# Filter spectra of a Hyena layer: three groups per order on TensorE in place of five, laid out by ScalarE, and an earlier second modulation trip

## What is computed

```python
def fft_long_conv(u, h, bias):
    L = u.shape[1]
    uf = u.astype(jnp.float32)
    spec = jnp.fft.rfft(uf, n=2 * L, axis=1) * jnp.fft.rfft(h, n=2 * L, axis=0)[None]
    y = jnp.fft.irfft(spec, n=2 * L, axis=1)[:, L // 2:L // 2 + L]
    return (y + uf * bias.astype(jnp.float32)).astype(u.dtype)

def hyena(u, conv_w, conv_b, w1, b1, w2, b2, w3, freq, bias):
    u = short_conv(u, conv_w, conv_b)
    v, x1, x2 = jnp.split(u, 3, axis=-1)
    h = implicit_filters(L, w1, b1, w2, b2, w3, freq)
    z = x1 * fft_long_conv(v, h[0], bias[0])
    return x2 * fft_long_conv(z, h[1], bias[1])

# per layer: scale, shift and gate vectors
mod_l = jnp.split(s_lat @ w_mod[l] + b_mod[l], N_MOD, axis=-1)
hl = modulate(rmsnorm(xl, norm1_g[l]), mod_l[0], mod_l[1])
```

## Time and profile before

| | us |
|---|---|
| time before, median of 3 runs (1947.94 to 1949.6) | 1948.33 |
| the profiled execution, its own time | 1946.0 |
| its span in the profile | 1944.1 |
| of it TensorE busy | 1884.3 (97%) |
| VectorE busy | 626.0 (32%) |
| ScalarE busy | 460.1 (24%) |

### The profile page before, as it was taken

The page is one execution under the profiler, slowest core; times in us unless marked ns, Lnnn a source line. Parts: engine busy times, 40 slices in busy tenths (PEclk is TensorE's granted clock), DMA queues, the critical chain, the costliest instruction groups (busy, mean ns, idle before and its releaser), DMA issues.

```text
span 1944.1 us, 43452 instructions
## 1 busy us (share of the span) xinstructions
PE 1884.3 (97%) x20106; PEld 1373.3 (71%) x20106; DVE 626.0 (32%) x892; ACT 460.1 (24%) x626; POOL 43.4 (2%) x53
## 2 busy tenths in 40 slices
PE   8999999999899999999998899999999999999997
PEld 3677776787688887776877886656666666666765
DVE  3545456444423332226645651001010111101012
ACT  4221144332433342114314441000000000000001
POOL 0000000002000001100000010000000000000000
PEclk9999999999999999999999998999999999999999
DMA  9721111126122326732332388999999999999991
GB/s 367 295 103 43 69 66 65 55 90 247 45 107 86 108 73 269 315 112 94 123 110 76 119 322 350 365 397 354 365 371 381 389 369 376 343 401 361 409 349 45
DMA packets 65489, 436.73 MB, mean 225 GB/s; under 512 B 7264, under 2 KB 8416, under 8 KB 21792
## 3 DMA queue, kind: packets, MB, share of 16 engines
q1 hardware_dynamic: 60992, 405.07, 54.6%
q0 software_dynamic: 4320, 28.96, 3.8%
HBM read 432.95 MB, written 1.05 MB: 223 GB/s over the span
## 4 chain that ended last, share of the span: by engine, by line
PE 87%; DVE 6%; DMA 3%; ACT 2%; issue 2%; SPq 0%; POOL 0%; DVEq 0%; ACTq 0%
PE psum L1878 24%; PE psum L1400 12%; PE psum L1923 11%; PE psum L1402 11%; PE psum L1401 11%; PE psum L1594 2%; PE psum L1447 2%; PE psum L1600 2%; DMA mod_units_e<-in_w_mod 1%; DVE squares L977 1%; PE psum L1518 1%; DVE h_lo L970 1%; PE psum L1635 1%; PE psum L1657 1%; PE psum L1853 1%
## 5 line engine op out<-in xcount | busy, mean ns | idle before, releaser
L1878 PE MATMUL psum<-expert_units,gathered 128*32 128x256 f32 (+1 forms) x9216 | 469.5, 363 | 1.1 <-issue 1.0
L1878 PEld LDWEIGHTS psum<-expert_units,gathered 128*32 128x32 f32 x9216 | 303.1, 110 | 154.9 <-issue 7.2
L1400 PE MATMUL psum<-h_hi,units_hi 128*128 128x512 f32 (+1 forms) x928 | 346.2, 373 | 13.0 <-DVE h_lo L970 5.9
L1402 PE MATMUL psum<-h_hi,units_lo 128*128 128x512 f32 (+1 forms) x928 | 334.9, 361 | 0.0
L1401 PE MATMUL psum<-h_lo,units_hi 128*128 128x512 f32 (+1 forms) x928 | 334.8, 361 | 0.0
L924 DVE TENSOR_TENSOR units_lo<-raw_units,units_hi 128x2048 fp32r<-128x2048 f32 (+2 forms) x88 | 175.1, 1991 | 322.4 <-ACT units_hi L564 322.3
L564 ACT ACTIVATE units_hi<-raw_units 128x2048 fp32r<-128x2048 f32 (+2 forms) x88 | 147.2, 1673 | 483.5 <-PE psum L1402 421.9
L1923 PE MATMUL psum<-expert_units,expert_midT 128*32 128x256 f32 x4080 | 225.3, 379 | 0.0
L1400 PEld LDWEIGHTS psum<-h_hi,units_hi 128*128 128x128 f32 x928 | 175.3, 189 | 53.2 <-issue 19.6
L1402 PEld LDWEIGHTS psum<-h_hi,units_lo 128*128 128x128 f32 x928 | 175.5, 189 | 27.2
L1923 PEld LDWEIGHTS psum<-expert_units,expert_midT 128*32 128x32 f32 x4080 | 135.8, 110 | 83.0 <-issue 1.0
(11 more groups left out here) (268 smaller groups left out, 2008.4 us busy)
## 6 DMA issues: line engine op xcount, KB each, us to landing
expert_units<-in_moe_up SPq DMA_DIRECT2D x128, 1024.0 KB, 8.1
expert_units<-in_moe_w SPq DMA_DIRECT2D x88, 1024.0 KB, 6.8
expert_units<-in_moe_up_rest SPq DMA_DIRECT2D x64, 768.0 KB, 5.1
raw_units<-in_w_in SPq DMA_DIRECT2D x40, 1024.0 KB, 4.9
raw_units<-in_ffn_w SPq DMA_DIRECT2D x22, 1024.0 KB, 4.9
mod_units<-in_w_mod POOLq DMA_DIRECT2D x20, 1024.0 KB, 10.4
raw_units<-in_ffn_w SPq DMA_DIRECT2D x16, 704.0 KB, 4.8
raw_units<-in_w_pab SPq DMA_DIRECT2D x16, 512.0 KB, 3.5
```

The lines of the kernel that those rows point to most:

```text
L1400: MM(o, wh, xh, start=first, stop=False)
L1402: return MM(o, wl, xh, start=False, stop=last)
L1878: ins = MM(o[GRP * q:GRP * (q + 1), :], G[:, k, at, GRP * s:GRP * (s + 1)], W[:, kk, c, :], start=k == 0 and rr % 2 == 0, stop=k == DK - 1 ...
```

## The change

Only three groups per order are computed on TensorE, six per layer: the real low bins (g = 0), the imaginary low bins with the Nyquist bin in row 0 (g = 1), and the high bins, real in the upper 64 rows and imaginary in the lower 64 (g = 2). ScalarE lays out the five tables from them in 8 instructions per order. The matrix `dftk` shrinks from 9 to 7 blocks of 64 columns (576 to 448 KB), the seventh being a column of ones with a zero in row 0, which is the scale that clears row 0 of table 1. TensorE's order in layer 0 becomes: spectra 0 and 1, trip 0, spectrum 2, turn 0, trip 1, spectrum 3, turn 1, spectra 4 and 5. ScalarE's order changes too. The wait for all copies ahead of `hyena_inputs` is split: layer 0 waits for two copies before it, both layers for four and for two copies after the first product, and for all of them after the stage.

```diff
             def spectrum_out(l, q):
-                act.wait_ge(f_pe, 11 * l + 4 + q)
-                A(spec[:, q // 5, q % 5, :], PS[:, spectrum_bank(l, q), :], ACT.Copy).then_inc(f_ac, 1)
+                act.wait_ge(f_pe, 7 * l + 4 + q)
+                o, g = q // 3, q % 3
+                bins = PS[:, spectrum_bank(l, q), :]
+                if g == 0:
+                    A(spec[:, o, 0, :], bins, ACT.Copy)
+                    A(spec[:, o, 2, :], bins, ACT.Copy).then_inc(f_ac, 1)
+                elif g == 1:
+                    A(spec[:, o, 1, :], bins, ACT.Identity, scale=dftks[l][:, 0, 6 * HALF:6 * HALF + 1])
+                    act.wait_ge(f_ac, 6 * l + 4 + q)
+                    A(spec[0:1, o, 2, :], bins[0:1, :], ACT.Copy).then_inc(f_ac, 1)
+                else:
+                    A(spec[0:HALF, o, 3, :], bins[0:HALF, :], ACT.Copy)
+                    A(spec[HALF:BINS, o, 3, :], bins[0:HALF, :], ACT.Copy)
+                    A(spec[0:HALF, o, 4, :], bins[HALF:BINS, :], ACT.Copy, scale=-1.0)
+                    A(spec[HALF:BINS, o, 4, :], bins[HALF:BINS, :], ACT.Copy).then_inc(f_ac, 1)
...
-                    for q in range(5):
+                    for q in range(4):
                         spectrum_out(0, q)
                     hi(0, 0, 0)
-                    for q in range(5, 7):
-                        spectrum_out(0, q)
+                    early = 4
+                else:
+                    spectrum_out(l, 0)
+                    norm_root(2)
+                    for q in range(1, 3):
+                        spectrum_out(l, q)
+                    early = 3
+                for q in range(early, 6):
+                    norm_hi(2 * l, SHIFT1, HH, 2 * (q - early), 2)
+                    spectrum_out(l, q)
+                norm_hi(2 * l, SHIFT1, HH, 2 * (6 - early), 6)
+                if l == 0:
                     hi(1, 1, 0)
-                    early = 7
-                else:
-                    for q in range(2):
-                        spectrum_out(l, q)
-                    norm_root(2)
-                    for q in range(2, 5):
-                        spectrum_out(l, q)
-                    early = 5
-                for q in range(early, 10):
-                    spectrum_out(l, q)
-                    norm_hi(2 * l, SHIFT1, HH, 2 * (q - early), 2)
-                norm_hi(2 * l, SHIFT1, HH, 2 * (10 - early))
+                norm_hi(2 * l, SHIFT1, HH, 2 * (9 - early))
...
@@ hyena_inputs, after the first product
+                    if n == 0:
+                        pe.wait_ge(f_ac, 4 + 6 * l + 4 - 2 * l)
...
@@ filter_spectra
-                    if l and q == 6:
-                        pe.wait_ge(evac, evb[0]["down"] + DK)
-                    reuse = 8 if l else 6
-                    if q >= reuse:
-                        pe.wait_ge(f_ac, 10 * l + 5 + q - reuse)
-                    o, g = q // 5, q % 5
+                    o, g = q // 3, q % 3
...
@@ TensorE's order in layer 0
             mod_turn(0, 0)
-            filter_spectra(0, 3, 6)
             mod_units(0, 1)
-            filter_spectra(0, 6, 7)
+            filter_spectra(0, 3, 4)
             mod_turn(0, 1)
-            filter_spectra(0, 7)
+            filter_spectra(0, 4)
...
-                pe.wait_ge(f_ac, 10 * l + 14)
+                if l == 0:
+                    pe.wait_ge(f_ac, 4 + 2)
                 hyena_inputs(l)
+                pe.wait_ge(f_ac, 4 + 6 * (l + 1))
```

More of the change, by code:

```diff
@@ L177, in build @@
         decays = [place("decay0", 59, [P, 2, 2, HY_W]), place("decay1", 88, [P, 2, 2, HY_W])]
[L178 removed]
+        dftks = [place("dft_filter0", 79, [P, 2, 7 * HALF]), place("dft_filter1", 96, [P, 2, 7 * HALF])]
         taps = place("filter_taps", 67, [P, 2, 2, HY_W])
@@ L1492, in filter_taps, with filter_spectra @@
                 last.then_inc(f_pe, 1)
-            def filter_spectra(l, first=0, end=10):
+            def filter_spectra(l, first=0, end=6):
                 for q in range(first, end):
@@ L1504, in filter_spectra @@
                         pe.wait_ge(n_rt, 2 * l + 1)
-                    if l and q == 6:
-                        pe.wait_ge(evac, evb[0]["down"] + DK)
-                    reuse = 8 if l else 6
-                    if q >= reuse:
-                        pe.wait_ge(f_ac, 10 * l + 5 + q - reuse)
-                    o, g = q // 5, q % 5
-                    for c in range(2):
-                        if g == 3:
-                            for h in range(2):
-                                last = MM(PS[h * HALF:(h + 1) * HALF, bank, :], dftks[l][:, c, 6 * HALF:7 * HALF], tapss[l][:, o, c, :],
-                                          start=c == 0, stop=c == 1)
-                        else:
-                            f = 7 * HALF if g == 4 else g * BINS
-                            last = MM(PS[:, bank, :], dftks[l][:, c, f:f + BINS], tapss[l][:, o, c, :],
-                                      start=c == 0, stop=c == 1)
+                    o, g = q // 3, q % 3
+                    for c in range(2):
+                        last = MM(PS[:, bank, :], dftks[l][:, c, g * BINS:(g + 1) * BINS], tapss[l][:, o, c, :],
+                                  start=c == 0, stop=c == 1)
                     last.then_inc(f_pe, 1)
@@ L2064, in tables @@
     imn[:, 0] = nyq
-    ren = re[:, :BINS].copy()
-    ren[:, 0] = nyq
     low, high = slice(0, BINS), slice(BINS, nbins)
     fwd = np.concatenate([re[:, low], imn[:, low], re[:, high], im[:, high], im[:, high], re[:, high]], axis=1)
-    fil = np.concatenate([re[:, low], (im * (k > 0))[:, low], ren, re[:, high], -im[:, high], im[:, high]], axis=1)
+    past_dc = np.repeat(np.arange(L) > 0, HALF).reshape(L, HALF)
+    fil = np.concatenate([re[:, low], imn[:, low], re[:, high], im[:, high], past_dc], axis=1)
     n = (np.arange(L) + L // 2)[None, :]
```

5 lines of the change are left out of this document (2 added, 3 removed).

## The result

The change makes the kernel slower. Its median is 1955.36 us over 10 executions (1950.82 to 1960.76) against 1948.49 for the kernel before, measured together with it (10 executions, 1945.65 to 1950.95); the ratio is 1.0033 [1.0023, 1.0043], the brackets being its 95% interval. A second batch gave 1953.30 against 1948.93, ratio 1.0030 [1.0019, 1.0041]. So the change costs 4 to 7 us; I had forecast 2.3, and 1953.1 as the upper end.

A forecast was written before the change was run, and what follows sets the result against it. It took VectorE's and ScalarE's chain of norm items as the bound, not TensorE. Layer 0 (0.5 + 2.3 + 1.2 = +4.0) and layer 1 (-3.0 + 1.3 = -1.7) gave +2.3: 1948.33 to 1950.6 us, range 1947.7 to 1953.1.

The forecast's parts named there:

- TensorE is not the bound: Both layers: the four groups saved, some 7.3 us of TensorE per layer, are worth nothing by themselves.
- Trip 1 waits for its fourth unit until 35.5, ends at 39.1: Layer 0: the fourth unit's load holds trip 1, so of 5.5 us earlier only 1.6 are left.
- hi of unit 0, +0.5: Layer 0, ScalarE: hi stands behind spectrum 3's copies, so VectorE's low of unit 0 starts at 44.0 in place of 43.50.
- ScalarE's copies: Layer 0, between norm items: copies of spectrum 4 cost 0.05, of spectrum 5 1.2; with hi of unit 1, +2.3 us.
- the wait ahead of item 10: Layer 0: hi of unit 1, moved between norm items 9 and 10, makes VectorE wait 1.05 us.
- the third rival: ScalarE's narrow copies are cheap, half of 0.59, so the median is 1948.4 us; chance 0.13.
- Layer 1, -3.0 and +1.3: Layer 1's norm chain starts 3.0 us earlier, and copies of spectra 4 and 5 among the items cost 1.3; net -1.7.
- The clock behind the first gap, +1.2: Layer 0: TensorE, nearly idle from 31.6 to 35.5, likelier than not falls to 1.2 GHz afterwards; +1.2 us, bounds 0 and 1.7.
- The second rival: Layer 0: the clock stays low through trip 1 and spectrum 3, costing 3.4 in place of 1.2; 1952.8 us, chance 0.17.
- a fall in the second gap: Layer 0: a clock fall between the end of spectrum 5 and the first norm items, 3.7 us, is hidden behind VectorE.
- Every stretch outside the terms of the sum at nothing: Rest of the kernel: only shifts with trip 2 and adds no time of its own; 0.3 us allowed in the range.
- a stretch elsewhere moves: Anywhere outside the changed stretches: listed as one of the ways the prediction would be wrong, given no size.

The follow-up runs named there:

- hifirst: The changed kernel with ScalarE's high part of unit 0 placed ahead of the copy of spectrum 3, TensorE's order kept; 1951.75 us, ratio 1.0012.
- thin_before: The kernel before with the matmuls of the last groups of spectra 8 columns wide in place of 512; 1947.80 us against 1948.68, ratio 0.9996.
- two_copies: The changed kernel with two full ScalarE copies in place of the four half-height ones of the high bins; 1951.70 us, ratio 1.0012.
- q3first: The changed kernel with spectrum 3 ahead of trip 1 again; 1949.13 us, ratio 1.0006.
- shifted: The changed kernel with 20 unused 8-column matmuls between the transposes of trip 0 and trip 1, moving the code packets; 1954.80 us, ratio 1.0036.

## Why the prediction was wrong, point by point

**TensorE is not the bound: right.** 3.8 us less of it, none of it gained.

**Trip 1 waits for its fourth unit until 35.5, ends at 39.1: right,** 35.41 and 39.0.

**hi of unit 0, +0.5: right.** Copies at 41.00 (41.1 forecast), low of unit 0 at 43.98 (44.0). hifirst shows it as the cause, and that 2.1 were to be had there.

**ScalarE's copies: the price was too low.** I took neighbours to overlap by 0.1 each, from two full copies in the earlier trace rows. The four copies of 64 rows start 0.59 to 0.61 apart: 2.41 in place of 2.06. The wait ahead of item 4 is 1.56, with a step of 1.65 in the chain, where I had 1.2 and 0.05; the wait ahead of item 10 is 0.95 (1.05). Together +2.7 (2.3). The page "ScalarE: Activation LUTs" of the Trainium skill, section "What ACT_TABLE_LOAD costs", gives an overlap of 93 ns for instructions back to back; full copies show it (0.59 long, 0.48 apart), the four narrow ones, each reading or writing other rows than the one before it, don't. That 64 rows cost as much as 128 was right, and so the third rival falls.

**Layer 1, -3.0 and +1.3: right in kind.** -3.0 (5.69 to 2.69 at the first low) and +1.7 in place of +1.3, the same four copies. Net -1.3 in place of -1.7. Sum of the work so far: 0.5 + 2.7 - 1.3 = +1.9, forecast 0.5 + 2.3 - 1.7 = +1.1.

**The clock behind the first gap, +1.2: right as a mean, but it is two cases.** In half of the profiles 1.5 to 2.0, in half nothing. It makes some 0.9 of the median. The second rival, a long stretch at the low clock, did not occur. That a fall in the second gap is hidden was right (thin_before). For layer 1 the prediction had no term for the clock.

**Every stretch outside the terms of the sum at nothing: the step that failed.** The prediction has what ends trip 2 later "move the rest by the same time", and allows 0.3 us above the second rival for other places; "a stretch elsewhere moves" stands only among the ways to be wrong. The first half holds: hifirst lies 2.13 below the first trace of the changed kernel at 43.50 and 60.66, and 2.17, 2.28, 2.02 and 2.05 below it at 112.98, 737.86, 812.78 and 900.89. But the rest did not stay as it was. Terms at nothing measured, from the last line of the table: +0.5 in trips 3 and 4 (4.4 to 4.9), +1.2 from the falls near 380 and 484 (4.9 to 6.2), +0.8 in the load at 740 (6.2 to 7.0), and +0.4 behind the norm items of layer 1 (5.8 to 6.2). That is 2.9 us against 0.3. With the 2.8 of work and first gap, where 2.3 was forecast, it is 5.7, between the two differences of the medians, 4.4 and 6.9.

That agreement is not a proof: the work is shown by experiments (hifirst, two_copies, q3first), the 2.9 are means over three traces and four, and the same line of the table ends at 2.7. The sum was also drawn from one profile, and the quickest of four: it had none of the falls near 1105 and 910 and the shortest one near 1170. Open are why the falls near 380 and 484 are likelier, what lengthens trips 3 and 4 (in shifted alone of the kernels with the changed order, where the code packets fall elsewhere, this step is -0.5), how much of the load at 740 is the packet, and what the experts give back.

## What to carry to other kernels

Before moving an instruction on an engine that feeds a chain of short items, count what may stand between two items without being seen (here 1.17 us on ScalarE), and place the rest behind the chain's consumers, not between its items or right behind it. Together with spectrum 3 ahead of trip 1 and hi of unit 1 ahead of the items, and with the same six groups per layer, that turned 0.3% slower into 0.2% faster. Fill an idle time on TensorE ahead of a stretch on the path with work that is wanted anyway, and where VectorE's chain hides a low clock, look how far the low clock reaches beyond the chain. And take more than one profile of the kernel before, because a low clock or a long load that is missing in one of them will be put down to the change.

## What the runs showed of the hardware that I had not expected

One gap of TensorE, in the same kernel, at the same place and of the same length, was followed by matmuls at 1.2 GHz in one execution and at 2.4 GHz in the next; over the executions of the changed kernel the time went up by 1.2 to 2.2 us for each 0.001 less of mean granted clock. A fall of 10.2 us in layer 1 cost 0.0 to 0.1 us where it ended with the norm items, and 1.1 to 1.3 us where it ended 2.5 to 2.9 us behind them. Four ScalarE copies of 64 rows cost 2.41 us where two of 128 rows cost 0.96. A 4 MB load that takes 13.2 us took up to 15.2 where a 16 KB packet of code fell into it, and once 14.7 without one.
